# Masks and first gate weights loaded during prompt attention, and dilated keys loaded in memory order over 128 partitions

## The reference

```
mod  = silu(c) @ w_ada + b_ada                  # shift, scale, gate terms, 6 x 1024
proj = h @ w_in  -> q_A k_A v_A q_B k_B v_B forget_logits gate_A gate_B
# A: dilated windows, 3 head groups x 4 heads, (window, dilation) = (128,1) (512,4) (2048,16)
kv_all = concatenate([cache_a[g], new rows])     # 128, 512, 2048 cached rows a sequence
idx = lw + t - dilation * arange(window / dilation + 1)      # keys of sample query t
sc  = where(valid, einsum(q, kv_all[idx].k) / sqrt(64), -inf)
o   = softmax(sc) @ kv_all[idx].v ; groups combined by their softmax denominators
# B: forgetting attention over 16 pages of 128 keys a sequence, found by page_table
mix = (sigmoid(gate_A) * (o_A @ w_pa) + sigmoid(gate_B) * (o_B @ w_pb)) @ w_o
x   = x + gate1 * RMSNorm(mix) ; then routing and 32 SwiGLU experts
```

## Time and profile before

| | us |
|---|---|
| median of 3 runs | 1196.73 |
| the profiled execution's own time | 1199.27 |
| its span, first to last instruction | 1197.5 |
| TensorE busy | 1000.1 (84%) |
| VectorE busy | 379.9 (32%) |
| ScalarE busy | 206.0 |
| POOL busy | 187.3 |
| mean granted TensorE clock | 0.914 |

### The profile page before, as it was taken

The page is one execution under the profiler, slowest core; times in us unless marked ns, Lnnn a source line. Parts: engine busy times, 40 slices in busy tenths (PEclk is TensorE's granted clock), DMA queues, the critical chain, the costliest instruction groups (busy, mean ns, idle before and its releaser), DMA issues. The chain is left out here.

```text
span 1197.5 us, 17987 instructions
## 1 busy us (share of the span) xinstructions
PE 1000.1 (84%) x7324; PEld 585.3 (49%) x7324; DVE 379.9 (32%) x865; ACT 206.0 (17%) x509; POOL 187.3 (16%) x210
## 2 busy tenths in 40 slices
PE   3999999997897169979989997579977998777770
PEld 2444444444564046647656674136554554444430
DVE  3100033237751164516701771003451222100105
ACT  3000000014542011100020003001231211111114
POOL 0000033311200100022222311100003322212110
PEclk9999999999997589989989998669978999989995
DMA  9976666977787779998969984979187999999966
GB/s 339 355 278 248 249 248 248 326 244 255 256 212 168 207 240 213 289 349 322 370 231 334 364 320 151 391 266 341 57 325 269 364 370 383 379 393 394 397 256 237
DMA packets 98062, 348.48 MB, mean 291 GB/s; under 512 B 13018, under 2 KB 56802, under 8 KB 78654
## 3 DMA queue, kind: packets, MB, share of 16 engines
q1 hardware_dynamic: 80478, 265.90, 64.8%
q0 software_dynamic: 15552, 79.97, 18.1%
q10 hardware_dynamic: 1952, 1.48, 0.5%
HBM read 335.46 MB, written 63.36 MB: 333 GB/s over the span
## 5 line engine op out<-in xcount | busy, mean ns | idle before, releaser
L1605 PE MATMUL bank<-turned,w_all 128*128 128x320 f32 (+1 forms) x512 | 143.7, 425 | 0.0
L442 PE MATMUL bank<-w_all,turned 128*128 128x481 f32 (+2 forms) x384 | 119.3, 503 | 1.1 <-DVE turned L651 1.1
L442 PE MATMUL bank<-w_ring,turned 128*128 128x481 f32 (+2 forms) x384 | 118.4, 502 | 0.0
L2013 PE MATMUL bank<-w_all,mix_row 128*64 128x256 f32 x736 | 92.2, 407 | 26.9 <-DMA w_all<-in_w_exp 25.8
L1605 PEld LDWEIGHTS bank<-turned,w_all 128*128 128x128 f32 x512 | 95.3, 196 | 35.6 <-issue 15.5
L2013 PEld LDWEIGHTS bank<-w_all,mix_row 128*64 128x64 f32 x736 | 60.9, 147 | 65.3 <-issue 46.4
L1709 DVE STREAM_TRANSPOSE mods<-w_all 128x2048 f32<-128x2048 f32 (+1 forms) x39 | 86.6, 2239 | 9.8 <-PE bank L1481 7.1
L442 PEld LDWEIGHTS bank<-w_all,turned 128*128 128x128 f32 (+1 forms) x384 | 56.8, 171 | 61.5 <-issue 58.3
L442 PEld LDWEIGHTS bank<-w_ring,turned 128*128 128x128 f32 (+1 forms) x384 | 57.1, 171 | 60.4 <-issue 57.3
L2059 DVE COPY act_t<-bank 128x128 f32<-128x128 f32 x33 | 9.6, 292 | 200.8 <-PE bank L2023 199.1
L661 DVE COPY w_all<-bank 128x481 f32 (+5 forms) x32 | 16.9, 531 | 152.6 <-PE bank L442 152.4
(11 more groups left out here) (357 smaller groups left out, 1318.5 us busy)
## 6 DMA issues: line engine op xcount, KB each, us to landing
w_all<-in_w_exp SPq DMA_DIRECT2D x22, 2048.0 KB, 41.0
out_a_sample<-in_cache_a SPq DMA_DIRECT2D x8, 4080.0 KB, 21.4
w_all<-in_w_exp SPq DMA_DIRECT2D x25, 1024.0 KB, 39.2
mods<-in_w_ada SPq DMA_DIRECT2D x21, 1024.0 KB, 8.8
w_all<-in_cache_a SPq DMA_DIRECT2D x96, 128.0 KB, 7.5
w_all<-in_cache_a SPq DMA_DIRECT2D x40, 256.0 KB, 6.1
turned<-in_w_exp SPq DMA_DIRECT2D x5, 2048.0 KB, 42.2
mods<-in_w_exp SPq DMA_DIRECT2D x5, 2048.0 KB, 43.7
```

Source lines behind the costliest of these rows:

```text
L442: mm = nc.tensor.matmul(m.banks[i][r:r + ROWS[i], 0:hi - lo], m.hT[:, k, i * P:i * P + ROWS[i]], ring[u][:, CW * k + lo:CW * k + hi], star ...
L1605: mm = nc.tensor.matmul(GATE[:, 0:WIDTH[h]], gate_w[b][k][:, c % 2 * P:(c % 2 + 1) * P], m.hT[:, k, 256 * h:256 * h + WIDTH[h]], start=k = ...
L2013: mm = nc.tensor.matmul(m.banks[2 + p][x * SLOTS:(x + 1) * SLOTS, 0:HID], hgT[:, k, :], m.weights(u)[:, (2 * k + x) * HID:(2 * k + x + 1) ...
```

## The change

1. `window_keys_in` issues 2 DMAs a step instead of 8, each over 128 partitions: partition 32 j + i now has row (i, c, t) of its sequence, so that partitions follow memory order. Runs stay 1 KB and bytes the same. The slot's order becomes (c, t).
2. The scores then come out of TensorE in another order. `add_bias` for a-units now adds per step of 256 columns (7 adds instead of 4, plus the one for new keys), reading the bank with a stride of 64 columns in runs of 4 and writing in place order; `peak` is 8 wide.
3. The window mask is tiled to 128 rows on the host and loaded in one DMA of 128 partitions in phase B, behind the keys of step 2 and `piece(13)`.
4. Gate weights of round 0 (2 x 1 MB) are issued in phase B, behind that mask (after a wait for the last turn of q and k) and behind `piece(14)`; merge weights of round 0 behind `piece(15)`. The slices move so that they leave the values of head group 0 alone.
5. In phase C the page rows of line 1833 are computed at the step of the first values (step 7), the wait for the mask and constants is at the adds, and the filler pieces start at step 1 (`FIRST, END = 1, 80`).

```diff
@@ window_keys_in
-    for j in range(4):
-        src = I[name][4 * u + j].rearrange("(c i t) n -> i t c n", c=4, t=t)[:, t0:t0 + n, :, 0:AH * HD]
-        dst = slot[32 * j:32 * j + 32, 0:n * 4 * AH * HD].rearrange("p (t c n) -> p t c n", t=n, c=4)
-        for x in range(n):
-            eng.dma_start(dst[:, x], src[:, x]).then_inc(arrived, 16)
+    src = I[name][4 * u:4 * u + 4].rearrange("s (i c t) n -> (s i) t c n", c=4, t=t)[:, t0:t0 + n, :, 0:AH * HD]
+    dst = slot[:, 0:n * 4 * AH * HD].rearrange("p (c t n) -> p t c n", t=n, c=4)
+    for x in range(n):
+        eng.dma_start(dst[:, x], src[:, x]).then_inc(arrived, 16)
+
+def gate_weights_in(eng, I, m, p, b):
+    src = I["w_gates"][2 * b + p // 2].rearrange("p (k n) -> p k n", k=KD)[:, :, (p % 2) * 256:(p % 2 + 1) * 256]
+    for lo, hi in ((0, 6), (6, 8)) if b == 0 else ((0, 4), (4, 8)):
...
+        eng.dma_start(dst.rearrange("p (k n) -> p k n", n=256), src[:, lo:hi, :]).then_inc(m.gate_in[b], 16)
@@ phase_b, SyncE
             for k in range(1, KV_RING - 1):
                 early_keys(k)
                 piece(BEFORE + 1 + k)
+                if k == 2:
+                    sp.dma_start(m.wmask, I["mask_window"]).then_inc(m.mask_in, 16)
+                    sp.wait_ge(turn_a, len(turns))
+                    sp.wait_ge(turn_d, len(turns))
+                    gate_weights_in(sp, I, m, 0, 0)
+                if k == 3:
+                    gate_weights_in(sp, I, m, 0, 1)
+            merge_weights_in(sp, I, m, 0)
@@ phase_c
-    FIRST, END = 3, 80
+    FIRST, END = 1, 80
@@ phase_c, SyncE
             window(KV_RING - 1)
-            gate_weights(0, 0)
-            for j in range(4):
-                sp.dma_start(wmask[32 * j:32 * j + 32, :], I["mask_window"]).then_inc(con_in, 16)
             sp.dma_start(consts[:], I["sample_consts"]).then_inc(con_in, 16)
-            gate_weights(0, 1)
-            merge_weights(0)
@@ phase_c, VectorE, add_bias
-                    cols = slice(512 * c, 512 * c + (512 if c < 3 else P))
-                    ins = add(sc_a[:, cols], S(u, c)[:, 0:cols.stop - cols.start], wmask[:, cols], peak[:, 0, c:c + 1])
+                    dve.wait_ge(m.mask_in, 16)
                     if c == 3:
+                        dve.wait_ge(con_in, 16)
+                    for g in (2 * c, 2 * c + 1) if c < 3 else (6,):
+                        lo, w = g % 2 * 256, P if g == 6 else 256
+                        by_key = lambda x: x.rearrange("p (y c) -> p y c", c=4)
+                        ins = add(by_key(sc_a[:, 256 * g:256 * g + w]), S(u, c)[:, lo:lo + w].rearrange("p (c y) -> p y c", c=4),
+                                  by_key(wmask[:, 256 * g:256 * g + w]), peak[:, 0, g:g + 1])
@@ phase_c, VectorE
             turn(0)
-            dve.wait_ge(pages_in, 16 * 2)
-            for j in range(4):
...
-            dve.wait_ge(con_in, 16 * 5)
             for t in range(N + 1):
...
+                    if (u, part, g) == (0, "v", 0):
+                        rows_of_pages()
```

More of the change, by code:

```diff
@@ L115, in build @@
         m.low = [m.qkv[:, i, 0:RING_AT] for i in range(TILES)]
+        m.wmask = m.low[4][:, 0:13 * P]
         m.sc = m.spare[:, 0:2 * (PAST + NS)]
@@ L129, in build @@
         m.wp_in, m.wo_in = [ctx.enter_context(nc.semaphore(n)) for n in ("w_p", "w_o")]
+        m.gate_in = [ctx.enter_context(nc.semaphore(f"gate_w{b}")) for b in range(2)]
+        m.merge_in, m.mask_in = [ctx.enter_context(nc.semaphore(n)) for n in ("merge_w", "mask_rows")]
         with ExitStack() as attn:
@@ L214, in constants @@
             "over_ids": np.arange(EXPERTS, BLOCKS, dtype=np.float32)[None, :],
-            "mask_window": np.concatenate(window, axis=1), "sample_consts": sample_consts,
+            "mask_window": np.tile(np.concatenate(window, axis=1), (4, 1)), "sample_consts": sample_consts,
             "page_consts": np.concatenate([before, seq_of, tri8], axis=1),
@@ L247, in window_keys_in, with merge_weights_in @@
     n = min(t, 2)
-    for j in range(4):
-        src = I[name][4 * u + j].rearrange("(c i t) n -> i t c n", c=4, t=t)[:, t0:t0 + n, :, 0:AH * HD]
-        dst = slot[32 * j:32 * j + 32, 0:n * 4 * AH * HD].rearrange("p (t c n) -> p t c n", t=n, c=4)
-        for x in range(n):
-            eng.dma_start(dst[:, x], src[:, x]).then_inc(arrived, 16)
+    src = I[name][4 * u:4 * u + 4].rearrange("s (i c t) n -> (s i) t c n", c=4, t=t)[:, t0:t0 + n, :, 0:AH * HD]
[5 more added lines that the diff above has]
+    for lo, hi in ((0, 6), (6, 8)) if b == 0 else ((0, 4), (4, 8)):
+        at = (8 * b + lo) % 6
+        dst = m.low[(8 * b + lo) // 6][:, at * 256:(at + hi - lo) * 256]
+        eng.dma_start(dst.rearrange("p (k n) -> p k n", n=256), src[:, lo:hi, :]).then_inc(m.gate_in[b], 16)
+def merge_weights_in(eng, I, m, p):
+    cols = slice(256 * p, 256 * (p + 1))
+    for name, lo, hi in (("w_pa", 16, 18), ("w_pb", 18, 22)):
+        dst = m.low[lo // 6][:, lo % 6 * 256:(lo % 6 + hi - lo) * 256].rearrange("p (k n) -> p k n", n=256)
+        eng.dma_start(dst, I[name].rearrange("p (k n) -> p k n", n=D)[:, :, cols]).then_inc(m.merge_in, 16)
 def window_values_in(eng, I, slot, arrived, u, g):
@@ L1177, in phase_c @@
         filled = from_pages if kind(u) == "b" else from_window
-        filled[slot_of[n]] += 16 * (1 if kind(u) == "b" else 8 if part == "k" and g < 6 else 4)
+        filled[slot_of[n]] += 16 * (1 if kind(u) == "b" else 4 if part == "v" else 2 if g < 6 else 1)
         level.append(filled[slot_of[n]])
@@ L1259, in phase_c @@
         run_id, pt_col = sb("run_ids", [P, 1], I32), sb("pages_col", [P, 1], I32)
-        peak = sb("chunk_max", [P, 2, 5])
+        peak = sb("chunk_max", [P, 2, 8])
         nm = sb("neg_max", [P, 2])
@@ L1264, in phase_c @@
         share = sb("shares", [P, 4])
-        wmask = m.low[4][:, 0:AT * P]
+        wmask = m.wmask
         osb = m.own_b[:, :, :, :].rearrange("p a f q -> p (a f q)").rearrange("p (s n) -> p s n", s=4)
@@ L1269, in phase_c @@
         sc_b = m.sc.rearrange("p (h n) -> p h n", h=2)
-        slices = [m.low[i][:, 256 * x:256 * (x + 1)] for i in range(4) for x in range(7)]
+        slices = [m.low[i][:, 256 * x:256 * (x + 1)] for i in range(4) for x in range(6)]
         gate_w = [slices[0:8], slices[8:16]]
         wp_a, wp_b = slices[16:18], slices[18:22]
-        th_a = {x: slices[22 + x] for x in range(4)}
-        th_b = slices[26:28]
+        th_a = {x: m.low[x][:, 1536:1792] for x in range(4)}
+        th_b = slices[22:24]
         flat_wa = m.wa[:].rearrange("p u f q -> p (u f q)")
@@ L1296, in phase_c @@
         bias_in = [sem(f"bias{x}") for x in range(4)]
-        gate_in, wp_in = [sem(f"gate_w{b}") for b in range(2)], sem("merge_w")
+        gate_in, wp_in = m.gate_in, m.merge_in
         gain_in, terms, terms_out = sem("gains"), sem("terms"), sem("terms_out")
@@ L1339, in gate_weights @@
             def gate_weights(p, b):
[L1340 to L1345, removed]
-            def merge_weights(p):
[L1348 to L1355, removed]
+                sp.wait_ge(gate_pe, sum_of[(2 * p - 1, 1, b)] + 1)
+                gate_weights_in(sp, I, m, p, b)
+            def merge_weights(p):
+                sp.wait_ge(out_pe, 4 * p)
+                merge_weights_in(sp, I, m, p)
             def past_bias(u, x):
@@ L1590, in piece @@
                     i = items.index((c, h))
-                    pe.wait_ge(wp_in, 48 * (c // 2 + 1))
+                    pe.wait_ge(wp_in, 32 * (c // 2 + 1))
                     pe.wait_ge(gated, 2 * i)
@@ L1722, in add_bias @@
                 if kind(u) == "a":
-                    cols = slice(512 * c, 512 * c + (512 if c < 3 else P))
-                    ins = add(sc_a[:, cols], S(u, c)[:, 0:cols.stop - cols.start], wmask[:, cols], peak[:, 0, c:c + 1])
+                    dve.wait_ge(m.mask_in, 16)
                     if c == 3:
-                        ins = add(sc_a[:, AT * P:AT * P + GROUPS * NS], S(u, c)[:, P:P + GROUPS * NS], mask_a[:, own(u), :], peak[:, 0, 4:5])
+                        dve.wait_ge(con_in, 16)
[4 more added lines that the diff above has]
+                                  by_key(wmask[:, 256 * g:256 * g + w]), peak[:, 0, g:g + 1])
+                    if c == 3:
+                        ins = add(sc_a[:, AT * P:AT * P + GROUPS * NS], S(u, c)[:, P:P + GROUPS * NS], mask_a[:, own(u), :], peak[:, 0, 7:8])
                 elif c < 4:
@@ L1739, in maxima @@
                 for h in range(1 if kind(u) == "a" else 2):
-                    V.tensor_reduce(nm[:, h:h + 1], peak[:, h, :], AX, ALU.max, negate=True).then_inc(mx, 1)
+                    V.tensor_reduce(nm[:, h:h + 1], peak[:, h, 0:8 if kind(u) == "a" else 5], AX, ALU.max, negate=True).then_inc(mx, 1)
             def recips(u):
@@ L1826, in _, with rows_of_pages @@
             use_dve = {"shares": shares, "fold": out_cols, "totals": past_sums}
-            turn(0)
-            dve.wait_ge(pages_in, 16 * 2)
-            for j in range(4):
```

(9 more changed lines are left out.)

## The result

The changed kernel takes 1153.1 us (median of 4 runs, 1148.4 to 1154.1) against 1196.7: a ratio of 0.9625, 95% interval 0.9587 to 0.9663, 43.6 us less. The forecast was 1156.5, range 1144 to 1177. The profiled execution has a span of 1151.6 us, 45.9 less than before.

What follows compares the result with a forecast made beforehand. The prediction took in-order issue of loads at the boundary into phase C as the bound. Terms of -27.3, -5 and -8 gave -40.3 us, taking the median from 1196.7 to about 1156.5 us, range 1144 to 1177.

Steps and rivals of the forecast that it cites:

- What bounds the kernel: At the boundary into phase C, in-order issue: a whole list of loads ahead of two small ones the first turn awaits.
- Term A: Boundary into phase C: with loads and waits moved, score 1 starts at 399.7 instead of 427.0; -27.3 us, bounds -30 and -24.
- The sign that I had named: Boundary into phase C: score 1 within 3 us after score 0 would show Term A.
- Filler at step 1: Start of phase C: only moves three pieces of the same 80 forward; costed at nothing.
- Term B: Phase B with moved loads and new keys: 300 GB/s taken, end at 389.8, -5 us; cases from -10 to +7.
- The sign that the DMA engines would still be busy from 381 to 390 us: End of phase B: DMA still busy at 381 to 390 would show Term B.
- Term C: The two a-units of phase C: faster keys shorten the queue and its waits; -8 us, bounds -13 and +3.
- The sum: Whole kernel: -27.3 - 5 - 8 = -40.3 us, median from 1196.7 to about 1156.5 us.
- The adds: VectorE in the a-units: more adds and a strided bank read hidden in slack; taken at 0, bounds 0 and +2.
- Rival 1: Keys stay at 206 GB/s because 1 KB runs at long HBM strides are slow; -25.5, 1171 us; chance 0.18.
- Rival 2: Phase B: moved loads delay pieces 14 and 15, +7 there, rest as forecast; -28, 1168 us; chance 0.12.
- Rival 3: Key loads: memory order is bad for HBM, so slower than before; +27, 1224 us at 110 GB/s; chance 0.05.

Runs made afterwards that it cites:

- e2: The kernel before with only VectorE's waits moved and its loads in their old order; 1185.6 us, 0.9896 of the kernel before.
- e3: The changed kernel with mask, gate and merge weights of round 0 issued in phase C behind `run_ids`; 1169.1 us, 0.9765 of the kernel before.
- e9: The changed kernel, unaltered, measured a second time; 1151.0 us, 0.9612 of the kernel before.
- e1: The changed kernel with the key loads (8 DMAs a step, 32 partitions each) and adds of before; 1182.4 us, 0.9859 of the kernel before.
- e8: The changed kernel with the second megabyte of round 0 gate weights issued behind piece 15 instead of piece 14; 1144.9 us, 0.9539 of the kernel before.
- e10: The same kernel as e8, measured again on one chip beside e9; 1145.9 us, 0.9566 of the kernel before.
- e5: The kernel before with only the new key loads and the adds that go with them; 1175.2 us, 0.9787 of the kernel before.

## Why the prediction was right, point by point

- **What bounds the kernel.** Right: the hole was an in-order list of loads, which two waits of VectorE stood behind. Moved waits let scores 1 and 2 follow at once (e2). What the reading of the boundary left out is that the hole covered other waits for the same list: gate weights 8.5 us and constants 15.3 in e2, gates 16.6 in e3. The change needs the early issue for its gain at this place.
- **Term A, -27.3.** Score 1 came 22.2 us earlier after score 0 (29.6 before, 7.4 now), but with the filler of step 1 in between. The sign that I had named, score 1 within 3 us, did not come: I had counted the pieces moved forward and forgotten that two of them stand between scores 0 and 1. At the last keys of unit 0 the gain is 23.6 us, with two filler pieces more done (2.0 to 2.4 each): 28 us at equal work. Right in size.
- **Filler at step 1, 0.** Right in the sum; its first 16 matmul records took 5.6 us, mostly at half clock, where the first 16 before took 3.7: 1.9 us, within the 3 that I left.
- **Term B, -5, bounds -10 and +7.** -8.9, within the bounds, 3.9 more than the value taken (4.3 more than the unrounded 4.6). The term that was mis-sized is the rate r: I took 300 GB/s, by which piece 15 is used 37.8 us behind the first issue; it was 34.6 (347.68 to 382.26), 328 GB/s. That is 3.2 of the 4.3. The other 1.1 is the work behind piece 15, 8.7 us in the sum and 7.6 here, at a granted clock of 0.91 from 381 to 390 us. That part is luck: in e9, the same kernel with the same 34.6 us, it ran at a granted clock of 0.50 from 381 to 391 us and the term was -5.6. That piece 15 would set the end was in the model, and it did, by 1.5 us. The sign that the DMA engines would still be busy from 381 to 390 us did not come (their share was 0.20, and from 385 to 390 us they moved 3 GB/s), since the loads were in sooner.
- **Term C, -8, bounds -13 and +3.** From the last keys of unit 0 to the first b score: 97.6 before, 82.5 now, 15.1 less; with the two filler pieces that were done before it, 11. The 7.1 us stall is gone, and so is the half clock behind it. 3 more than the value taken and inside the bounds, same mechanism.
- **The sum, -40.3.** The two stretches gave 47.6, 7.3 more. That the median came within 3.4 us of the forecast is partly chance: the changed trace entered the first stretch 4.4 us later than the trace before, which is spread and not part of the model, and e9 stood 45.9 under the runs of the kernel before that were made beside it.
- **The adds, 0.** Adds of 128x256 with a strided bank read took 0.39 to 0.42 us, as the contiguous ones of 418 ns. The 92 ns I allowed for the stride do not show.
- **Rival 1 (keys no faster, -25.5).** Its mechanism is false, and e1, which makes it true, shows that its price was wrong: -14 to -17, not -25.5. A and C of this rival came out (-26.3 in the a-units); what was wrong is B. I let the other transfers run at 300 GB/s beside keys at 206; in e1 the tail moved 258 GB/s from 355 to 365 us and grew by 12.3 us over the kernel before, where I had +2. The loads queued behind the slow keys came late: piece 15 was used 52.5 us behind the first issue, against 34.6 in the changed kernel.
- **Rival 2 (the moved loads delay pieces 14 and 15).** True where keys are slow (15.7 us of waiting in e1), and in small in the changed kernel: 1.5 to 4.1 us, of which 1.2 is left in e8 and e10.
- **Rival 3 (memory order bad for HBM).** No sign: 46 ns a packet, with partitions 128 KB apart.

## What to carry to other kernels

When an engine stands still at a phase boundary with transfers running, read the issue queue from the small load that it waits for back to its start: the wait can be moved, but what else hides in the hole must be issued earlier too, and how much that pays depends on the transfer time that the phase before has left (16 us here with the new keys, about 3 with the old ones). Compare transfers by time per packet, not only by GB/s: here one DMA over 128 partitions took a third off each 1 KB packet, with the same bytes and the same runs. Loads moved into an earlier phase are better issued behind that phase's own last load than between its loads: piece 15 was used 3 us earlier by it.

## What the runs showed that was not expected

- A 1 KB packet took 69 to 73 ns in DMAs of 32 or 64 partitions and 46 to 47 ns in DMAs of 128, whatever the source order or the size of the DMA.
- In prompt attention the two halves of the change depend on each other: the tail of B is 12.3 us longer with the early loads alone (e1), 9.2 shorter with fast keys alone (e5), and 8.9 shorter with both. In the whole time the surplus over the sum (-22 to -26, -14 to -17, -44 to -45 together) is not clear of the intervals.
- Two traces of one kernel with the same loads differ by 3.3 us in the tail, by where TensorE's half clock falls (changed and e9).
- Four loads of gate weights issued at the start of a phase took 12.4 to 15.9 us to land (e3), where 8 to 10 was worked out from bytes.
